# The sample states' recurrence moves from beside the prompt attention to beside the sample attention, and two matmul loops are turned

## The reference

```python
sp = einsum('bqhcd,bkhcd->bhcqk', q, k_past) * ATT_SCALE      # c: the two halves of a head
sn = where(tril, einsum('bqhcd,bkhcd->bhcqk', q, k) * ATT_SCALE, -inf)
p = softmax(concatenate([sp, sn], -1), -1)
wgt = p[:, :, 0] - lam * p[:, :, 1]
o = einsum('bhqk,bkhd->bqhd', wgt, concatenate([v_past, v]))
```

```python
sa = einsum('bhvk,bhk->bhv', s, -kk_t)
s = s * w_t + sa[..., None] * (kk_t * a_t) + v_t[..., None] * k_t
y = einsum('bhvk,bhk->bhv', s, r_t)
```

## Time and profile before

| what | value |
|---|---|
| median of 3 runs | 2587.2 us (2583.82 to 2591.53) |
| profiled execution, its own time | 2592.17 us |
| its span, first to last instruction | 2590.6 us |
| PE busy | 2092.7 us (81%) |
| DVE busy | 1241.9 us (48%) |
| ACT busy | 833.8 us (32%) |
| POOL busy | 564.4 us (22%) |
| granted TensorE clock, mean | 0.884 |

### The profile page before, as it was taken

How to read it: one execution, slowest core, us unless ns; L and a number is a source line. 1 busy time by engine, 2 the same in 40 slices (tenths; PEclk the granted TensorE clock), 3 DMA queues, 4 the chain that set the end, 5 groups by cost and what they waited for, 6 DMA issues and landing times. The chain is left out here.

```text
span 2590.6 us, 35820 instructions
## 1 busy us (share of the span) xinstructions
PE 2092.7 (81%) x13340; PEld 1962.7 (76%) x13340; DVE 1241.9 (48%) x1952; ACT 833.8 (32%) x1407; POOL 564.4 (22%) x679
## 2 busy tenths in 40 slices
PE   1999954449999863446599549999999998999997
PEld 1999953348898862445366449999999998999997
DVE  5010125645655428986111126665555556355476
ACT  3111123213334312335100125443333334344454
POOL 0000002341322129970221111211111111010022
PEclk9999985679999855677788669999999999999998
DMA  2222232000000022212664216321111112555434
GB/s 104 85 97 84 99 120 70 34 26 1 0 0 0 0 46 66 49 42 57 205 202 126 87 51 229 101 64 50 41 50 48 43 50 66 167 162 161 145 116 131
DMA packets 71624, 211.89 MB, mean 82 GB/s; under 512 B 11506, under 2 KB 17570, under 8 KB 71218
## 3 DMA queue, kind: packets, MB, share of 16 engines
q1 hardware_dynamic: 55986, 156.30, 19.6%
q0 software_dynamic: 13344, 48.59, 5.4%
q10 hardware_dynamic: 2176, 5.42, 0.7%
HBM read 179.04 MB, written 31.24 MB: 81 GB/s over the span
## 5 line engine op out<-in xcount | busy, mean ns | idle before, releaser
L2002 PE MATMUL bh_acc<-Mh,bh_wh 128*128 128x352 f32 x2016 | 658.3, 327 | 34.0 <-DVE bh_wl L2272 28.3
L2002 PE MATMUL bh_acc<-Ml,bh_wh 128*128 128x352 f32 x2016 | 650.8, 323 | 0.0
L2002 PE MATMUL bh_acc<-Mh,bh_wl 128*128 128x352 f32 x2016 | 650.8, 323 | 0.0
L2002 PEld LDWEIGHTS bh_acc<-Mh,bh_wh 128*128 128x128 f32 x2016 | 382.1, 190 | 36.8 <-DVE bh_wl L2272 29.7
L2002 PEld LDWEIGHTS bh_acc<-Ml,bh_wh 128*128 128x128 f32 x2016 | 383.2, 190 | 0.0
L2002 PEld LDWEIGHTS bh_acc<-Mh,bh_wl 128*128 128x128 f32 x2016 | 381.7, 189 | 0.0
L2272 DVE TENSOR_TENSOR bh_wl<-bh_raw,bh_wh 128x1024 fp32r<-128x1024 f32 x170 | 201.2, 1184 | 166.3 <-ACT bh_wh L2077 166.2
L403 PE MATMUL in_acc<-Hh,in_wh 128*128 128x352 f32 x624 | 202.1, 324 | 24.5 <-DVE in_wl L386 24.5
L2077 ACT ACTIVATE bh_wh<-bh_raw 128x1024 fp32r<-128x1024 f32 x170 | 174.0, 1024 | 119.7 <-PE bh_acc L2002 106.6
L403 PE MATMUL in_acc<-Hl,in_wh 128*128 128x352 f32 x624 | 200.6, 321 | 0.0
L403 PE MATMUL in_acc<-Hh,in_wl 128*128 128x352 f32 x624 | 200.4, 321 | 0.0
(11 more groups left out here) (328 smaller groups left out, 3774.4 us busy)
## 6 DMA issues: line engine op xcount, KB each, us to landing
bh_raw<-dram_w_down SPq DMA_DIRECT2D x48, 512.0 KB, 3.7
bh_raw<-dram_w_up SPq DMA_DIRECT2D x44, 512.0 KB, 3.6
as_kT<-dram_k_pool SPq DMA_DIRECT2D x64, 256.0 KB, 4.6
as_vp<-dram_v_pool POOLq DMA_DIRECT2D x64, 256.0 KB, 4.1
dram_projT<-in_out POOLq DMA_DIRECT2D x26, 528.0 KB, 3.0
in_raw<-dram_w_in SPq DMA_DIRECT2D x26, 512.0 KB, 3.6
bh_raw<-dram_w_o SPq DMA_DIRECT2D x24, 512.0 KB, 3.9
bh_raw<-dram_w_gate SPq DMA_DIRECT2D x24, 512.0 KB, 3.7
```

The costliest lines, as they stand in the source:

```text
L2002: ins = mm(out, w(k), x, start=first and k == 0 and q == 0, stop=last and k == len(xs) - 1 and q == 2)
```

## The change

`attend_prompt` no longer takes `beside`; POOL's queue is empty in it. `attend_sample` takes two of them. `recur` is split: POOL does rows 0 to 15 of the 32 with the same operations, DVE rows 16 to 31, with tensor_reduce for the two sums in the place of the halving, so 9 operations a token, 36 in all (`DVE_STEPS`). DVE's are handed out one at a time by a generator: one ahead of the wait for the scores, one ahead of the wait for the exponential, two ahead of the wait for the summed values, what is left at the end. DVE's loop over samples is written out, with the same order of fronts and backs. The pick of the queries moves from POOL to DVE, to the head of front(n). The V pages move from POOL's queue to ACT's, ahead of the exponential of the same sample. On TensorE the two loops are turned: scores go by half and then by head, values by page and then by head.

```diff
-        @block.gpsimd
-        def _(pool):
-            beside(pool, beside_done)
...
+            beside_pool(pool, pool_step)
...
-                for h in range(HEADS):
-                    for j in range(PAGES + 1):
+                for j in range(PAGES + 1):
+                    for h in range(HEADS):
...
-                for h in range(HEADS):
-                    rows = slice(32 * h, 32 * h + 32)
-                    for half in range(2):
-                        last = nc.tensor.matmul(sc[rows, half * 512:(half + 1) * 512], qb[:, b, h, :],
-                                                kT[:, b, half * 4:half * 4 + 4, h, :], start=True, stop=True)
...
+                for half in range(2):
+                    for h in range(HEADS):
+                        nc.tensor.matmul(sc[rows(h), half * 512:(half + 1) * 512], qb[:, b, h, :],
+                                         kT[:, b, half * 4:half * 4 + 4, h, :], start=True, stop=True)
...
+            def front(n, b):
+                nc.vector.tensor_copy(qb[:, b], qd[:, n]).then_inc(S["q_picked"], 1)
+                next(beside, None)
                 dve.wait_ge(S["scored"], n + 1)
...
+                next(beside, None)
                 dve.wait_ge(S["exped"], n + 1)
...
+                next(beside, None)
+                next(beside, None)
                 dve.wait_ge(S["summed"], n + 1)
...
+            for last in beside:
+                pass
+            dve.wait_ge(dve_step, DVE_STEPS)
...
+            act.wait_ge(S["table_in"], 16)
+            pages(act, 0, 0, vp, a["v_pool"], v_in)
+            pages(act, 1, 1, vp, a["v_pool"], v_in)
             step(0, 0, True)
             step(1, 1, True)
             with act.Fori(1, NB // 2) as i:
                 for b in range(2):
+                    act.wait_ge(S["summed"], i * 2 + b - 1)
+                    pages(act, i * 2 + b, b, vp, a["v_pool"], v_in)
                     step(i * 2 + b, b, False)
...
+    def steps(self, rows, tmp, summed):
...
+        for t in range(NT):
+            yield tmp, st, along_v(t, 1), ALU.mult
+            yield from summed(tmp, sav)
+            yield st, st, along_v(t, 0), ALU.mult
+            yield tmp, along_k(sav), along_v(t, 2), ALU.mult
+            yield st, st, tmp, ALU.subtract
+            yield tmp, along_k(v2[:, t]), along_v(t, 3), ALU.mult
+            yield st, st, tmp, ALU.add
+            yield tmp, st, along_v(t, 4), ALU.mult
+            yield from summed(tmp, ys[:, t])
```

More of the change, by code:

```diff
@@ L444, in run_units, with attend_prompt @@
         step(HEADS // 2, u)
-def attend_prompt(kit, proj, oT, ident, identb, causal, neg_lam, beside):
+def attend_prompt(kit, proj, oT, ident, identb, causal, neg_lam):
     nc = kit.nc
@@ L465, in attend_prompt @@
     head_out = [kit.sem(f"ap_head_out{b}") for b in range(2)]
-    beside_done = kit.sem("ap_beside_done")
     SCALE = DH ** -0.5
@@ L684, in _, with attend_sample @@
             run_units(act, ((keep_v, 0), (exponential, 0), (keep, 2), (leave, 3), (split, 0)))
-def attend_sample(kit, a, proj, oT, ident, identb, neg_lam_rows):
+def attend_sample(kit, a, proj, oT, ident, identb, neg_lam_rows, beside_pool, beside_dve):
     nc = kit.nc
@@ L701, in attend_sample @@
     v_in = [kit.sem(f"as_v_in{b}") for b in range(2)]
+    pool_step, dve_step = kit.sem("as_pool_step"), kit.sem("as_dve_step")
     with ExitStack() as ctx:
@@ L808, in back @@
                             v, w = vnew[:, h, :], wT[0:NS, b, j, h, :]
-                        last = nc.tensor.matmul(pv[32 * h:32 * h + 32, 0:P], w, v, start=(j == 0), stop=(j == PAGES))
+                        last = nc.tensor.matmul(pv[32 * h:32 * h + 32, 0:P], w, v, start=(j == 0), stop=(j == PAGES),
+                                                skip_group_check=True)
                 last.then_inc(S["summed"], 1)
@@ L816, in front @@
                     pe.wait_ge(S["exped"], n)
-                for h in range(HEADS):
-                    rows = slice(32 * h, 32 * h + 32)
-                    for half in range(2):
-                        last = nc.tensor.matmul(sc[rows, half * 512:(half + 1) * 512], qb[:, b, h, :],
-                                                kT[:, b, half * 4:half * 4 + 4, h, :], start=True, stop=True)
-                    last = nc.tensor.matmul(sc[rows, 1024:W], qb[:, b, h, :], qkv[:, 1, h, :],
-                                            start=True, stop=False, skip_group_check=True)
+                rows = lambda h: slice(32 * h, 32 * h + 32)
+                for half in range(2):
+                    for h in range(HEADS):
+                        nc.tensor.matmul(sc[rows(h), half * 512:(half + 1) * 512], qb[:, b, h, :],
+                                         kT[:, b, half * 4:half * 4 + 4, h, :], start=True, stop=True)
+                for h in range(HEADS):
+                    nc.tensor.matmul(sc[rows(h), 1024:W], qb[:, b, h, :], qkv[:, 1, h, :],
+                                     start=True, stop=False, skip_group_check=True)
                 nc.tensor.matmul(sc[:, 1024:W], identb, mask[:, ds(n * NS, NS)], start=False, stop=True,
@@ L847, in _ @@
             dve.wait_ge(S["w_zeroed"], 1)
+            dve.wait_ge(S["q_placed"], 2 * HEADS)
             dve.wait_ge(S["v_turned"], 1)
             nc.vector.tensor_copy(vnew[:].rearrange("p h c -> p (h c)"), vps[0:NS, :]).then_inc(S["v_kept"], 1)
-            def front(n, b, first):
+            beside = beside_dve(dve, dve_step)
+            def front(n, b):
+                nc.vector.tensor_copy(qb[:, b], qd[:, n]).then_inc(S["q_picked"], 1)
+                next(beside, None)
                 dve.wait_ge(S["scored"], n + 1)
@@ L862, in front @@
                 dve.wait_ge(S["scaled"], n + 1)
-                if not first:
+                if n >= 2:
                     dve.wait_ge(S["turned"], n - 1)
@@ L866, in front, with back @@
                                         ALU.mult).then_inc(S["combined"], 1)
-            def back(n, b, first):
+            def back(n, b):
                 dve.wait_ge(S["turned"], n + 1)
-                if not first:
+                if n >= 2:
                     dve.wait_ge(S["summed"], n - 1)
@@ L875, in back @@
                                       tokens(tp[0:NS, PAGES * 16:(PAGES + 1) * 16], 1)).then_inc(S["kept"], 1)
+                next(beside, None)
+                next(beside, None)
                 dve.wait_ge(S["summed"], n + 1)
[L877 to L891, removed]
+                nc.vector.tensor_copy(rows_out[:, n], pv[:, 0:P]).then_inc(S["evacuated"], 1)
+            front(0, 0)
+            for n in range(1, NB):
+                front(n, n % 2)
+                back(n - 1, (n - 1) % 2)
+            back(NB - 1, (NB - 1) % 2)
+            for last in beside:
+                pass
+            dve.wait_ge(dve_step, DVE_STEPS)
             dve.wait_ge(S["out_turned"], 1)
@@ L1543, in _ @@
             dve.wait_ge(S["y_added"], NCH)
+POOL_ROWS = 16
+DVE_STEPS = NT * 9
 class SampleStates:
@@ L1620, in _, with recur_pool, halving @@
                 dve.wait_ge(S["state_in"], 32)
[L1622 to L1628, removed]
+    def steps(self, rows, tmp, summed):
+        vec, n = self.vec, rows.stop - rows.start
+        v2, st, sav, ys = self.v2[:, :, rows], self.st[:, rows], self.sav[:, rows], self.ys[:, :, rows]
+        along_v = lambda t, q: vec[:, t, q, :].unsqueeze(1).broadcast_to([P, n, 64])
+        along_k = lambda z: z.unsqueeze(2).broadcast_to([P, n, 64])
+        for t in range(NT):
[8 more added lines that the diff above has]
+            yield from summed(tmp, ys[:, t])
+    def recur_pool(self, pool, done):
+        def halving(tmp, out):
             n = 32
@@ L1634, in summed, with recur_dve, reduced @@
             yield out, tmp[:, :, 0], tmp[:, :, 1], ALU.add
[L1636 to L1647, removed]
+        rows = slice(0, POOL_ROWS)
+        for n, (out, x, y, op) in enumerate(self.steps(rows, self.tmp[:, rows], halving)):
+            if n:
+                pool.wait_ge(done, n)
+            self.nc.gpsimd.tensor_tensor(out, x, y, op).then_inc(done, 1)
+    def recur_dve(self, dve, done):
+        def reduced(tmp, out):
+            yield out, tmp, None, ALU.add
+        rows = slice(POOL_ROWS, 32)
+        for n, (out, x, y, op) in enumerate(self.steps(rows, self.tmp[:, rows], reduced)):
+            if n:
+                dve.wait_ge(done, n)
+            if y is None:
+                yield self.nc.vector.tensor_reduce(out, x, AX, op).then_inc(done, 1)
+            else:
+                yield self.nc.vector.tensor_tensor(out, x, y, op).then_inc(done, 1)
     def unload(self, kit, o, ident, Y):
@@ L2669, in build @@
             states.load(kit, a["wkv"], o["sd"])
-            attend_prompt(kit, proj, oT, ident[:], identb[:], causal[:], lam[:, 4:5], states.recur)
+            attend_prompt(kit, proj, oT, ident[:], identb[:], causal[:], lam[:, 4:5])
             kit.retire()
```

(2 more changed lines are left out.)

## The result

The changed kernel takes 2489.97 us (median of 4 runs, 2484.41 to 2491.48) against 2587.45 for the kernel before beside it: a ratio of 0.9619, interval 0.9598 to 0.964, 97.5 us less. Predicted were 2498 us, within 2468 to 2538. The profiled execution's span fell from 2590.6 to 2487.3, and the stages account for these 103.3 us: the prompt attention, from its first load to the sample attention's table load, 73.5 less (208.0 against 281.5), the sample attention, from there to the copy into `as_out`, 28.9 less (151.1 against 180.0), the untouched stages ahead 5.0 less and those behind 4.0 more.

What follows compares the result with a forecast made beforehand. DVE, taking turns with POOL, was held to bound the prompt attention, TensorE the sample attention at 19.6 us a sample. Savings of 68.5 + 21 = 89.5 us turned 2592.2 into 2502.7; 5.0 lower for the median gave 2498, range 2468 to 2538.

Steps and rivals of the forecast that it cites:

- Part 1: Prompt attention: with POOL gone, DVE's subtractions take 1.22 us; start saves 11.6, heads 56.9, together 68.5 us.
- the lower bound: Prompt attention: head 0 takes 34 us instead of 39.7, having no units of an earlier head to finish.
- the 62 to 74: Prompt attention: bounds of the gain in us, 62 if head 0 takes 46, 74 if it takes 34.
- Part 2: Sample attention on TensorE, loops turned: four column groups at once at 1.2 GHz, scores 3.9 us, values 4.0.
- Rival A: Sample attention: only two column groups run at once, values 7.7 us, cycle 21, kernel 2528 us; chance 0.13.
- Part 3: Sample attention: eight V page issues on ACT ahead of the exponential, 9.9 us, form a chain from sample to sample.
- The 17.2: Sample attention: cycle per sample in us, taken between 17.5 with POOL's turn and 16.6 without.
- Rival D: Sample attention: ACT reads page numbers slowly; at 2.8 us a page all gain is used, at 3.2 2613 us; chance 0.03.
- Part 4: Sample attention: DVE's half of the recurrence and picks, with waits for POOL, make a 16.4 us chain, as long as ACT's.
- a sign of being wrong: Sample attention: scores waiting on the pick by more than 3 us a sample would show the prediction wrong.
- Rival B: Sample attention: DVE's waits for POOL become the bound, 22 us a cycle, stage 190, kernel 2528 us; chance 0.13.
- Rival C: Sample attention: TensorE stays at 2.4 GHz, POOL's turns miss the chain; cycle 14.9, kernel 2480 us; chance 0.18.

## Why the prediction was right

**Part 1.** The mechanism held: subtractions at 1.22, weights at their short times, and the load of Q and K late next in heads 1 to 3 (idle 7.25, 7.95 and 7.89 us against 7.8). The start saved 11.4 us (11.6). The heads were 35.5, 45.6 and 48.0 against 39.7, 47.5 and 47.5: the term mis-sized is head 0, by 4.2 us. It was put at a full head less DVE's idle of 7.8. But the wait costs more than that idle: with the earlier loads heads 1 and 2 came to 38.1. And head 0, at 35.8 there, lacks 2.3 more; it has no units of an earlier head to finish, which I had named for the lower bound and not taken. Saved in all 73.5, against 68.5, just within the 62 to 74.

**Part 2.** Four groups at once, as assumed beyond what the earlier trace rows showed. At 1.2 GHz scores with new keys and mask took 3.9 us (3.9), values 3.7 to 4.2 (4.0). Rival A's 7.7 fell.

**Part 3.** ACT's chain set the cycle, shown by the exchange of the two statements. The eight pages took 8.2 to 8.5 us from the first issue to the last, and 9.2 to 9.6, on the mean 9.3, from the end of the values to the exponential (in sample 2 from 1209.3 to 1218.57), against 9.9 in the sum: the term was 0.6 too large, most of what the cycle was, 16.45 against 17.2. The 17.2 was a choice and not the sum: the terms as written add to 17.7 with the turn, not 17.5, and the exponential and the comb stand in them with 2.4 us where the earlier trace rows give 2.0. Six cycles make 4.5 of the 7.9 us by which the stage was shorter than predicted (151.1 against 159, saved 28.9 against 21); the start, 40.7 to the first evacuation against 43 (its terms add to 43.9), makes 2.3, the tail the rest. Rival D wanted 2.8 us a page; sixteen in 16.50 at the stage's start settle it.

**Part 4.** DVE's chain was put level with ACT's (16.4 against 17.2; its terms add to 16.75) and waited for ACT little or not at all in four samples of eight; but in three it waited 3.5 to 4.8 us, so it was the shorter of the two. The groups of DVE in the changed kernel, sample attention only, mean ns of one:

```profile
L1663 DVE TENSOR_TENSOR rs_st<-rs_st,rs_tmp 128x1024 f32<-128x1024 f32 x8 | 12.5, 1563 | 0.1
L1663 DVE TENSOR_TENSOR rs_tmp<-rs_st,rs_vec 128x1024 f32<-128x1024 f32 x8 | 11.0, 1378 | 0.1
...
L1663 DVE TENSOR_TENSOR rs_tmp<-rs_sa,rs_vec 128x1024 f32<-128x1024 f32 x4 | 10.0, 2504 | 0.0
L839 DVE COPY as_qb<-as_qd 128x128 f32<-128x128 f32 x8 | 9.5, 1184 | 0.0
L855 DVE TENSOR_SCALAR as_combs<-as_comb,as_small 128x16 f32<-128x16 f32 x8 | 9.0, 1128 | 0.3
...
L1661 DVE TENSOR_REDUCE rs_y<-rs_tmp 128x16 f32<-128x1024 f32 x4 | 4.9, 1213 | 0.1
```

The pick at 1.18 and the comb at 1.13 (0.21 and 0.23 where nothing stood in the way) pay the 0.9 that I put on each. The steps pay 0 to 1.3 on average, less than 0.9 and 2.2 by turns. The reduces over SBUF, which no row of before showed beside POOL, pay nothing: five of the eight ran while POOL worked, and none took over 1.22. The Trainium skill, "SBUF - State Buffer", section Who interferes with whom, says so of tensor_reduce, and the trace agrees. Scores waiting on the pick by more than 3 us were named as a sign of being wrong, and it came twice: 3.9 and 4.1 us in samples 4 and 6, where the maximum was ready only as ACT's issues ended, so that DVE's chain stood level with ACT's there. Rival B fell with POOL's half left out: 0.9 us a cycle, where it wanted some 5. Rival C wanted 2.4 GHz throughout, and 0.67 was granted. POOL was done at 1285.4, 110 us after its first step (117), before the last three evacuations.

The sum of the steps, 89.5, stands against 73.5 + 28.9 = 102.4 in the two stages of the profile and 97.5 between medians. Five of the 13 us between them lie in heads 0 and 1, eight in the sample attention. What the prediction missed is where the gain of that stage lay: it gave 21 us for parts 2 to 4 together, and so did not say that the loops alone bring 64 (180 to 116) and that the recurrence, the pick and the V pages beside them take 35 back.

## What to carry to other kernels

Matmuls that write different groups of columns run side by side only as far as their order in the queue puts different groups next to each other (16 records in 1.92 us against 4 in 1.05), so the loop over groups goes innermost. Before issues of transfers are moved to an idle engine, look at what stands behind them in its queue: eight cheap page issues ahead of one exponential cost 19 us that an exchange of two statements gave back. And price a change stage by stage with each part alone; a part that makes a stage worse is hidden by one that makes it better.

## What the runs showed of the hardware

Eight page lookups with their issues took ACT 8.2 to 8.5 us, no more than SP's 8.57. Small DVE operations inside SBUF can pay POOL's turn in full: a copy of 128x128 took up to 2.16 us for 0.21, and a 128x16 scaling 2.25 for 0.23, both ending within 0.1 us of the POOL operation that had begun ahead of them. With the loops turned and nothing else changed, the page transfers reached 350 GB/s at a share of 0.97 over five cycles, where the kernel before moved 195 in this stage.
